# Half output blocks behind the weights of the last four heads, on the vector engine, in two attention layers

## The reference

```python
for i in range(DEPTH):                      # DEPTH = 2
    mod = silu_c @ ada_w[i] + ada_b[i]
    sh1, sc1, g1, sh2, sc2, g2 = ...
    h = rms_norm(x, norm_mix_g[i]) * (1.0 + sc1) + sh1
    y = diff_attention(h, ...) if i % 2 == 0 else chunked_attention(h, ...)
    x = x + g1 * y
    h = rms_norm(x, norm_ffn_g[i]) * (1.0 + sc2) + sh2
    x = x + g2 * grouped_moe(h, ...)
```

## Time and profile before

| | |
|---|---|
| median of 3 runs | 1739.26 us (1736.14 to 1740.77) |
| the profiled execution, its own time | 1736.32 us |
| its span | 1734.5 us |
| PE busy | 1617.4 us, 93% of the span |
| DVE busy | 473.0 us, 27% |
| ACT busy | 368.1 us, 21% |
| mean granted clock of PE | 0.961 |
| DMA | 535.17 MB, mean 309 GB/s |

### The profile page before, as it was taken

One profiled execution on the slowest core, in us unless ns is written; L12 is line 12 of the kernel. 1 busy time (PEld: TensorE's weight loads), 2 busy tenths in 40 slices (PEclk: granted clock), 3 DMA queues, 4 the chain that ended last, 5 costly groups with the idle time before them and its releaser, 6 DMA issues.

```text
span 1734.5 us, 20614 instructions
## 1 busy us (share of the span) xinstructions
PE 1617.4 (93%) x8418; PEld 901.9 (52%) x8418; DVE 473.0 (27%) x1118; ACT 368.1 (21%) x770; POOL 34.0 (2%) x44
## 2 busy tenths in 40 slices
PE   5999879999989988999998996897799999999998
PEld 3664654444465647444444782345644444444444
DVE  2044331212123234312122123463311212121212
ACT  2142221111122234211112311442211111111111
POOL 0000000000000000000000001040000000000000
PEclk9999989999999998999999996897799999999999
DMA  9996649999999567699998100004269999999995
GB/s 320 386 386 246 245 166 427 428 429 428 414 335 331 194 243 321 281 427 428 428 429 329 49 1 0 1 1 194 97 286 425 429 429 429 429 429 428 428 427 238
DMA packets 94672, 535.17 MB, mean 309 GB/s; under 512 B 7935, under 2 KB 11737, under 8 KB 69922
## 3 DMA queue, kind: packets, MB, share of 16 engines
q1 hardware_dynamic: 94258, 534.41, 75.8%
q10 hardware_dynamic: 368, 0.12, 0.0%
HBM read 533.44 MB, written 1.06 MB: 308 GB/s over the span
## 4 chain that ended last, share of the span: by engine, by line
PE 85%; DMA 5%; DVE 4%; SPq 2%; ACT 2%; issue 1%; DVEq 0%; POOL 0%; ACTq 0%
PE pair L901 24%; PE bank L890 7%; PE pair L908 6%; PE bank L630 6%; PE bank L908 6%; DMA ring<-in_w_dram 4%; PE bank L637 3%; PE bank L591 3%; PE bank L951 3%; PE pair L951 3%; PE bank L724 2%; SPq L403 1%; DMA ring<-in_a_w_qkv_dram 1%; PE bank L1047 1%; PE pair L1112 1%
## 5 line engine op out<-in xcount | busy, mean ns | idle before, releaser
L901 PE MATMUL pair<-ring,arena 128*64 128x512 f32 x2048 | 447.3, 594 | 3.5 <-DVE arena L1837 2.9
L901 PEld LDWEIGHTS pair<-ring,arena 128*64 128x64 f32 x2048 | 144.7, 137 | 288.1 <-issue 288.1
L890 PE MATMUL bank<-arena 128*128 128x128 f32 x1120 | 139.5, 279 | 9.4 <-DVE arena L1825 9.4
L1850 DVE TENSOR_TENSOR arena<-sq,pair 128x512 f32<-128x512 f32 x32 | 34.0, 1061 | 408.2 <-PE pair L901 408.2
L890 PEld LDWEIGHTS bank<-arena 128*128 128x128 f32 x1120 | 133.6, 196 | 9.9 <-issue 9.9
L630 PE MATMUL bank<-hh,ring 128*128 128x256 f32 x512 | 120.6, 394 | 6.9 <-ACT hh L1206 3.5
L908 PE MATMUL pair<-ring,arena 128*64 128x512 f32 x512 | 116.9, 598 | 0.0
L908 PE MATMUL bank<-ring,arena 128*64 128x512 f32 x512 | 115.3, 592 | 0.0
L630 PEld LDWEIGHTS bank<-hh,ring 128*128 128x128 f32 x512 | 99.4, 197 | 28.0 <-issue 11.6
L1376 ACT ACTIVATE sq<-pair 128x512 f32<-128x512 f32 x32 | 19.1, 597 | 370.3 <-PE pair L901 370.3
L1858 DVE COPY arena<-bank 128x512 f32<-128x512 f32 x32 | 22.1, 692 | 202.7 <-PE bank L908 202.7
(11 more groups left out here) (375 smaller groups left out, 1623.3 us busy)
## 6 DMA issues: line engine op xcount, KB each, us to landing
ring<-in_w_dram SPq DMA_DIRECT2D x96, 2048.0 KB, 15.6
ring<-in_moe_w_gate_dram SPq DMA_DIRECT2D x32, 2048.0 KB, 11.6
ring<-in_moe_w_up_dram SPq DMA_DIRECT2D x32, 2048.0 KB, 15.9
ring<-in_moe_w_down_dram SPq DMA_DIRECT2D x32, 2048.0 KB, 13.9
ring<-in_ada_w_dram SPq DMA_DIRECT2D x24, 2048.0 KB, 17.4
ring<-in_w_mod_dram SPq DMA_DIRECT2D x12, 2048.0 KB, 12.2
ring<-in_a_w_qkv_dram SPq DMA_DIRECT2D x6, 2048.0 KB, 19.2
ring<-in_b_w_qkv_dram SPq DMA_DIRECT2D x6, 2048.0 KB, 11.7
```

The costliest lines, as they stand in the source:

```text
L890: last = mm(b[part][:, cols(k % 4)], h_tok[:, t, cols(k)], pick[:, t, :], start=(t == 0), stop=(t == TT - 1))
L901: last = mm(b[2 + m][half(a), :], x_sel[:, k, half(a)], R8[moe_slot(l, a, m)][:, k, :], start=(k == 0), stop=(k == KT - 1))
L1850: tt(hid.rearrange("p (f q) -> p q f", f=FT), by_row(gate_act), by_row(b[3]), ALU.mult).then_inc(M["hid_ready"], 1)
```

## The change

Only the order in which DVE takes its steps in the second half of `attention_layer` changes, for both layers:

```diff
                 maxima(4)
                 maxima(5)
+                weights(4)
                 half_out(0)
-                weights(4)
                 maxima(6)
+                weights(5)
                 half_out(1)
-                weights(5)
                 maxima(7)
+                weights(6)
                 half_out(2)
-                weights(6)
+                weights(7)
                 half_out(3)
-                weights(7)
                 half_out(4)
                 half_out(5)
```

## The result

The changed kernel takes 1724.84 us (median of 4 runs, 1722.03 to 1725.08) against 1739.15 us before (4 runs, 1736.14 to 1740.77): ratio 0.9915, 95% interval 0.9901 to 0.993, 14.3 us less. Forecast were 1726.5 us and a gain of 12.3 us. The two profiled spans, 1734.5 and 1723.1 us, differ by 11.4 us.

The account below looks back on a forecast made before the run. PE was taken as the bound, 85% of the chain; removing its waits for DVE's weights, 7.2 + 5.1 = 12.3 us, gave 1724.0 or 1727.0 by baseline, with other terms at 0. Forecast 1726.5 us, range 1720 to 1734.

Parts of the forecast that it names:

- The waits go, all eight: In both attention layers' second halves, PE's transposes of heads 4 to 7 would no longer wait for DVE's weights.
- the margin of head 4: In layer 0, weights(4) would end at 166.3 and PE reach its transposes at 167.0: 0.7 us to spare.
- Their size, 7.2 + 5.1 = 12.3: PE's waits before the transposes, 7.2 us in layer 0 and 5.1 in layer 1, were the whole gain.
- the idle behind may be more: Matmul ends in the profile are modelled, so PE's idle might exceed the waits; a larger gain got chance 0.02.
- Chunks come in time: B[4] to B[7] would land as before, ahead of PE's use, margins 1.7 us upward; late chunk or Exp, chance 0.08.
- Half_outs at nothing: Delaying the eight half_outs on DVE would cost 0, at most 0.8 us.
- The expert loops keep their rhythm: Expert loop turns would not slow from 28.94 to 29.37 us; the rival, 11.2 us lost, got chance 0.06.
- The clock, 0 plus or minus 3: Stages behind the change, partly at 1.2 GHz, would shift; their clock cost was taken as 0, plus or minus 3 us.
- the base of 1736.3 us: The profiled execution of the kernel before, 1736.3 us; subtracting 12.3 gave 1724.0.
- leaning to the median: Three runs' median, 1739.26 us, gave 1727.0 by the same sum; the forecast, 1726.5, was put nearer to it.
- The landmarks: First expert issues were expected near 193.8 and 641.3 us, first L901 of the loops near 242.5 and 687.6.

Follow-up runs that it names:

- e1: Kernel before with the weights ahead of the half_outs in layer 0 only; 1729.78 us, ratio 0.9951.
- e5: Kernel before with DVE's order kept; PE instead takes mods(B[4]) to mods(B[7]) ahead of transposes(4) to transposes(7); 1727.24 us, ratio 0.9932.
- e3: Kernel before with only weights(4) and weights(5) moved ahead, in both layers; 1737.75 us, ratio 0.9989; repeated once for another profile, 1739.86 us.
- e4: Kernel before with only weights(6) and weights(7) moved ahead of half_out(2) and half_out(3), in both layers; 1730.13 us, ratio 0.9949.
- e7: Kernel before with half_out(0) and half_out(1) put behind weights(6), half_out(2) and half_out(3) behind weights(7); 1728.69 us, ratio 0.9943; repeated once, 1727.87 us.
- e0: The changed kernel run again without further change; 1723.89 us, ratio 0.9914 to the kernel before.
- e6: Changed kernel plus eight unread DVE reciprocals, one in front of each of the last four heads' weights per layer; 1732.66 us, ratio 0.997 to before.
- before_again: The kernel before, unchanged, run once more for a second profile; 1738.25 us.

## Why the prediction was right

- *The waits go, all eight.* Right, and the margin of head 4 was met to 0.1 us (0.7 against 166.71 - 165.98), those of the others in layer 0 to 0.3 us. e1 to e5 show that these waits, and not DVE's order as such, are the gain.
- *Their size, 7.2 + 5.1 = 12.3.* A little small: 7.76 + 5.67 = 13.4. The term is short by 1.1 us, 0.07 us for each wait of heads 4 and 5 and 0.2 us for each of heads 6 and 7: e3_again gives 2.87 against 2.74 in layer 0 and 1.82 against 1.70 in layer 1, e4 4.89 against 4.45 and 3.84 against 3.42. The rows show where it lies. A wait is counted from the modelled end of the last matmul, and a matmul that need not wait starts before that end: transposes(4) at 166.71 start 0.86 us after scores(6), whose row has 0.93 us, and transposes(6) start 1.83 us after out_first(2), whose row has 1.99 us. The prediction had named this ("the idle behind may be more") and gave it no size.
- *Chunks come in time.* Right in the outcome, with a wrong part: I took the landings as fixed. B[7] of layer 0 took 20.4 us to land in the changed kernel's profile, against 19.0, and its margin was 0.7 us, not 2.7. The later landing goes with an earlier use of B[4]: in the eight profiles in which mods(B[4]) start by 167.5 that time is 20.1 to 20.4 us, also in e5, whose DVE order is the old one, and in the five in which they start at 168.3 or later 18.8 to 19.2. So landings are not fixed by the issues alone. Why is open.
- *Half_outs at nothing.* Right for this order; e7 prices four half_outs put still later at 1.7 us.
- *The expert loops keep their rhythm.* Right: from the loop's first issue to the next layer's first chunk 202.35 us in layer 0 and 202.34 in layer 1, in before and after alike.
- *The clock, 0 plus or minus 3.* The sign was rightly left open, the size was too small and the place incomplete. I looked at the route stages; layer 0's took 56.1 to 59.9 us over the profiles, but the third layer alone ran 321.5 to 334.8 us. The 56.1 us are those of the first profile of before, the shortest of all, so the base of 1736.3 us was a fortunate execution, and leaning to the median was right. That the clock left the whole gain near the waits is luck: nothing in the forecast fixed it, and e3 ended 3.0 us short of its stretches. The third layer repeated to 0.6 us in each kernel that has two profiles (before 322.9 and 323.5, changed 321.5 twice, e3 327.7 and 327.8), so its time may follow the kernel's own timing as much as the execution; this is open. The rule from the Trainium skill (TensorE: Matmul & The Clock Gate, Part 1), that the gate's windows are free-running, fits that the same code differs between two executions of one kernel (58.3 and 56.1 us behind layer 0 in two profiles of before).
- *The landmarks.* The expert issues came at 192.96 and 642.95, forecast 193.8 and 641.3; the first L901 of the loops at 244.7 and 689.6, forecast 242.5 and 687.6: 0.8 us early by the waits, then some 2 us late by the clock.

13.4 us of the 14.3 are accounted for by the stretches. The remaining 0.9 is within the interval, and the spread of the clock is larger than that.

## What to carry to other kernels

On an in-order engine, put the step that the critical engine waits for ahead of a step whose result is wanted only later, if its inputs are already there; the gain is the sum of the critical engine's waits at that place, head by head, here with 0.07 to 0.2 us more for each. Check the new deadline of the step that was put back: here putting it back further cost 1.7 us. Measure such a change in a stretch between two fixed events of the profile, which repeats to 0.02 us where the clock stays at 1.00, since the whole run scatters by 2 to 15 us with the clock.

## What the runs showed of the hardware

- With PE unchanged in its work, the third layer's mixing part took from 321.5 us (92 us of it at half clock, e0) to 334.8 us (123 us at half clock, e6): about 0.43 us lost per us at half clock, by these two. In e3's stretch it was 3.25 us for 6.8, 0.48; in layer 0's route stage, of the changed kernel against before, 3.0 us for 10.2 us more at half clock, 0.3.
- The clock could fall for 3.4 us after a PE wait of 2.2 us (e3_heads_4_5, twice) or of 1.84 us, and did not in other executions with the same waits: at the 1.84 us in front of L740 in layer 0 it fell in six of the twelve profiles that have this wait, in the old order (before_again) as in the changed one.
- The fourth of five 2 MB transfers in a queue, issued at nearly the same place, landed 18.8 to 19.2 us after its issue in five profiles and 20.1 to 20.4 us after it in eight; in the five PE began to use the first of them at 168.3 us or later, in the eight by 167.5. The cause is open.
